# Four PSUM banks for scores and two for turned weights, the latent mask inside the rotary product, and GpSimd's splits in the softmax half

## The reference, cut to what matters

```python
# stick-breaking, strictly causal
z = q @ k.T * 64 ** -0.5
log_rem = where(causal, log_sigmoid(z) - z, 0)
w = where(causal, exp(log_sigmoid(z) + reverse_exclusive_cumsum(log_rem)), 0);  out = w @ v
# latent head: visible is by chunks of 64 tokens
s = (q_nope @ k_nope.T + q_rope @ k_rope.T) * 96 ** -0.5
s = where(k_pos // 64 <= q_pos // 64, s, lowest)
out = softmax(s) @ v
```

## Time and profile before

| | before |
|---|---|
| median of 3 runs | 2409.52 us |
| the profiled execution's own time | 2408.51 us |
| its span | 2406.7 us |
| granted TensorE clock, mean | 0.963 |
| TensorE products busy | 2178.7 us (91%) |
| TensorE weight loads busy | 1817.9 us (76%) |
| VectorE busy | 1348.9 us (56%) |
| ScalarE busy | 1277.0 us (53%) |
| GpSimd busy | 893.4 us (37%) |

### The profile page before, as it was taken

The page is one execution under the profiler, slowest core; times in us unless marked ns, Lnnn a source line. Parts: engine busy times, 40 slices in busy tenths (PEclk is TensorE's granted clock), DMA queues, the critical chain, the costliest instruction groups (busy, mean ns, idle before and its releaser), DMA issues. The chain is left out here.

```text
span 2406.7 us, 39504 instructions
## 1 busy us (share of the span) xinstructions
PE 2178.7 (91%) x12100; PEld 1817.9 (76%) x12100; DVE 1348.9 (56%) x2780; ACT 1277.0 (53%) x2616; POOL 893.4 (37%) x922
## 2 busy tenths in 40 slices
PE   6999998999989799789999999999999993999998
PEld 1888886999988477558686878787877771778886
DVE  3232332300128333278888888888888863667783
ACT  2222232311113333268888888888888873567553
POOL 0000000000000000164858585858585744656673
PEclk9999998999999999879999999999999995999999
DMA  7433332322347799934343434333333215676772
GB/s 277 138 100 100 96 119 79 127 73 73 120 156 203 232 313 309 280 83 99 72 99 68 100 69 96 75 90 78 85 79 83 62 32 143 191 224 179 218 214 88
DMA packets 296938, 320.10 MB, mean 133 GB/s; under 512 B 88642, under 2 KB 221789, under 8 KB 291827
## 3 DMA queue, kind: packets, MB, share of 16 engines
q1 hardware_dynamic: 292002, 302.00, 44.5%
q10 hardware_dynamic: 2880, 9.05, 1.0%
q0 software_dynamic: 1904, 7.41, 0.8%
HBM read 199.09 MB, written 110.90 MB: 129 GB/s over the span
## 5 line engine op out<-in xcount | busy, mean ns | idle before, releaser
L1437 ACT ACTIVATE pa_whi<-banks 128x512 fp32r<-128x512 f32 (+3 forms) x640 | 341.0, 536 | 119.1 <-PE banks L1675 104.8
L1675 PE MATMUL banks<-ident,pa_p 128*128 128x128 f32 x2176 | 350.0, 276 | 0.0
L1600 POOL TENSOR_TENSOR pa_wlo<-pa_whole,pa_whi 128x512 fp32r<-128x512 f32 (+2 forms) x240 | 276.6, 1171 | 135.2 <-ACT pa_whole L1442 135.0
L1658 PE MATMUL banks<-pa_khi,pa_qst 128*128 128x512 f32 (+3 forms) x640 | 257.8, 403 | 59.7 <-DVE pa_p L1503 51.3
L1675 PEld LDWEIGHTS banks<-ident,pa_p 128*128 128x128 f32 x2176 | 264.3, 141 | 54.3 <-issue 1.5
L1632 PE MATMUL banks<-pa_whi,pa_vst 128*128 128x512 f32 (+3 forms) x640 | 282.1, 441 | 17.4 <-POOL pa_wlo L1600 17.4
L1503 DVE TENSOR_TENSOR_SCAN pa_p<-banks,pa_p,pa_zero 128x512 f32<-128x512 f32 x192 | 246.3, 1283 | 64.4 <-ACT banks L1397 57.1
L1480 DVE TENSOR_TENSOR pa_wlo<-banks,pa_whi 128x512 fp32r<-128x512 f32 (+3 forms) x400 | 234.6, 586 | 28.3 <-ACT pa_whi L1437 27.3
L699 POOL DMA_DIRECT2D gate_ada<-in_ada_w_dram x2 | 1.8, 886 | 641.0 <-DVE qu_wlo L755 641.0
L1659 PE MATMUL banks<-pa_klo,pa_qst 128*128 128x512 f32 (+3 forms) x640 | 238.7, 373 | 0.0
L1632 PE MATMUL banks<-pa_wlo,pa_vst 128*128 128x512 f32 (+3 forms) x640 | 234.0, 366 | 0.0
(11 more groups left out here) (260 smaller groups left out, 5198.4 us busy)
## 6 DMA issues: line engine op xcount, KB each, us to landing
scratch_sb_kT<-ke_kT SPq DMA_DIRECT2D x12, 1024.0 KB, 9.1
scratch_mla_kT<-ke_nT SPq DMA_DIRECT2D x12, 1024.0 KB, 5.1
scratch_mla_v<-ke_v SPq DMA_DIRECT2D x12, 1024.0 KB, 5.4
scratch_gatesT<-co_gates SPq DMA_DIRECT2D x12, 704.0 KB, 11.3
ada<-in_ada_w_dram SPq DMA_DIRECT2D x4, 2048.0 KB, 12.3
pr_x<-in_x_prompt_dram SPq DMA_DIRECT2D x16, 512.0 KB, 18.8
scratch_hT<-pr_hT SPq DMA_DIRECT2D x16, 512.0 KB, 5.1
ke_k<-in_cache_sb_k_dram SPq DMA_DIRECT2D x8, 1024.0 KB, 7.6
```

The source lines that it names most:

```text
L1437: act.activation(whi[:, t % NW, q0:], bank, ACT.Copy).then_inc(hi_done, 1)
L1600: pool.tensor_tensor(wlo[:, t % NW, q0:], whole[:, t % 4, q0:], raw(whi[:, t % NW, q0:]), ALU.subtract).then_inc(pool_lo, 1)
L1658: pe.matmul(bank, qst[job][:, q], khi[job][:, keys], start=True, stop=False)
L1675: y = pe.transpose(ps[:, NS + t % NTB, x * P:(x + 1) * P], probs[g][x][:, i * P:(i + 1) * P], s["ident"][:])
```

## The change

It does four things. `NS` becomes 4 and `NTB` 2. The mask of the latent head gets 16 rows of its own in the rotary operands, one for each tile of 128 tokens (`krst` and `qrst` have 112 rows): key rows hold a very low number for the second 64 tokens of the tile, query rows a one for the first 64, so the rotary product adds the mask and the product with `hide` goes. GpSimd's splits lie in steps 22 to 61, in an order of parts by when the old ones are no longer read, with a semaphore for each of the four pieces; SP's loads move with them. At the start SP loads the mask's rows, and GpSimd copies them (and `own_tile`) where ScalarE and VectorE did before.

```diff
-    NS, NTB, NW = 2, 4, 5
+    NS, NTB, NW = 4, 2, 5
...
-        krst = sb("pa_krst", [3 * ROPE, T], F32R)
-        qrst = sb("pa_qrst", [3 * ROPE, T], F32R)
+        ROWS = 3 * ROPE + TILES
+        krst = sb("pa_krst", [ROWS, T], F32R)
+        qrst = sb("pa_qrst", [ROWS, T], F32R)
...
+        mask_rows = slice(3 * ROPE, ROWS)
+        half_rows = [x[mask_rows, 0:T // 2] for x in (probs[1][3][:], probs[2][2][:], probs[2][3][:], whole[:, 0:2].rearrange("p b n -> p (b n)"))]
+        hidden_keys, blind_queries = half_rows[0:2], half_rows[2:4]
+        own_raw = probs[1][0][:, 0:CH]
...
-        SPLITS = (((0, "v", 1), (6, 10, 14, 18)), ((1, "k", 0), (22, 26, 30, 34)), ((1, "v", 0), (46, 50, 54, 58)),
-                  ((1, "k", 1), (62, 66, 70, 74)))
+        SPLITS = (((1, "k", 0), ((0, 22), (1, 24), (2, 26), (3, 28))), ((0, "v", 1), ((0, 30), (1, 32), (2, 34), (3, 36))),
+                  ((1, "k", 1), ((3, 40), (2, 55), (1, 58), (0, 61))), ((1, "v", 0), ((3, 43), (2, 46), (1, 49), (0, 52))))
+
+        def part_order(name, job):
+
+            return [part for (_, *piece), parts in SPLITS if piece == [name, job] for part, _ in parts]
+
+        def left_by(name, job, part):
+
+            if job:
+                users = [G + k for k in range(G) if size_of(G + k) >= part]
+            else:
+                users = [k for k in range(G) if size_of(k) >= part]
+            return upto(max(users))
...
-                sp.dma_start(raw(krst[:]), d["mla_krT"][:, 0:T]).then_inc(kr_loaded, 16)
-                sp.dma_start(probs[2][3][:, 0:CH], d["const_own_tile"]).then_inc(own_loaded, 16)
+                sp.dma_start(raw(krst[0:3 * ROPE, :]), d["mla_krT"][:, 0:T]).then_inc(kr_loaded, 16)
+                sp.dma_start(own_raw, d["const_own_tile"]).then_inc(own_loaded, 16)
+                for i in range(2):
+                    at = slice(i * T // 2, (i + 1) * T // 2)
+                    sp.dma_start(hidden_keys[i], d["const_hidden_keys"][:, at]).then_inc(own_loaded, 16)
+                    sp.dma_start(blind_queries[i], d["const_blind_queries"][:, at]).then_inc(own_loaded, 16)
...
-                LOADS = {0: (load_k, 0), 18: (load_v, 0), 20: (load_q, 0), 34: (load_k, 1), 58: (load_v, 1), 60: (load_q, 1)}
+                LOADS = {0: (load_k, 0), 20: (load_q, 0), 30: (load_k, 1), 38: (load_v, 0), 54: (load_v, 1), 60: (load_q, 1)}
...
-                act.wait_ge(own_loaded, 16)
-                act.wait_ge(hide_made, 2)
-                act.activation(own_tile[:], probs[2][3][:, 0:CH], ACT.Copy)
-                act.activation(hide[:], probs[2][3][:, CH:CH + P + CHUNK], ACT.Copy).then_inc(const_done, 1)
+                act.wait_ge(const_done, 1)
...
-                hidden = probs[2][3][:, CH:CH + P + CHUNK]
-                dve.memset(hidden, 0.0).then_inc(hide_made, 1)
-                dve.wait_ge(hide_made, 1)
-                dve.memset(hidden[0:1, 0:CHUNK], 1.0)
-                dve.memset(hidden[0:1, P:], -BIG).then_inc(hide_made, 1)
...
-                    if part == 0:
+                    first = part == part_order(name, job)[0]
+                    if not (isinstance(h, int) and h == 0):
+
+                        if name == "v":
+                            wait_apart(pool, mixed, NW + HEAD * h + left_by(name, job, part), passed)
+                        else:
+                            wait_apart(pool, scores, HEAD * (h - 1) + left_by(name, job, part), passed)
+                    if first:
                         loaded, count = ((k_loaded, 32 * (2 * h + job + 1)) if name == "k" else
                                          (v_loaded, 80 * h + (80 if job else 64)))
                         wait_apart(pool, loaded, count, passed)
...
+                wait_apart(pool, own_loaded, 5 * 16, passed)
+                pool.tensor_copy(own_tile[:], own_raw).then_inc(row_made, 1)
+                for i in range(2):
+                    at = slice(i * T // 2, (i + 1) * T // 2)
+                    pool.wait_ge(row_made, 2 * i + 1)
+                    pool.tensor_copy(krst[mask_rows, at], hidden_keys[i]).then_inc(row_made, 1)
+                    pool.wait_ge(row_made, 2 * i + 2)
+                    pool.tensor_copy(qrst[mask_rows, at], blind_queries[i]).then_inc(row_made, 1)
+                wait_apart(pool, row_made, 5, const_done)
...
-                        if t in when and not (on and last):
-                            split(h + on, name, job, when.index(t))
+                        for part, at in when:
+                            if t == at and not (on and last):
+                                split(h + on, name, job, part)
...
-                        mm = pe.matmul(bank, qrst[:, q], krst[:, keys], start=False, stop=(c != g))
-                        if c == g:
-
-                            mm = pe.matmul(ps[:, m % NS, width - CHUNK:width], hide[:, 0:P], hide[:, P:],
-                                           start=False, stop=True)
+                        mm = pe.matmul(bank, qrst[:, q], krst[:, keys], start=False, stop=True)
...
+        "const_hidden_keys": np.where((tile == token // P) & (token % P >= CHUNK), f(-BIG), f(0.0)),
+        "const_blind_queries": ((tile == token // P) & (token % P < CHUNK)).astype(f),
```

More of the change, by code:

```diff
@@ L1175, in prompt_attention_phase @@
         const_loaded, const_done = sm.one("const_loaded"), sm.one("const")
-        kr_loaded, own_loaded, hide_made = sm.one("kr_loaded"), sm.one("own_loaded"), sm.one("hide_made")
+        kr_loaded, own_loaded, row_made = sm.one("kr_loaded"), sm.one("own_loaded"), sm.one("row_made")
         k_loaded, v_loaded, q_loaded = sm.one("k_loaded"), sm.one("v_loaded"), sm.pair("q_loaded")
-        kv_hi, kv_split = sm.one("kv_hi"), sm.one("kv_split")
+        PIECES = (("k", 0), ("v", 0), ("k", 1), ("v", 1))
+        kv_hi, kv_split = ({piece: sm.one(f"{what}_{piece[0]}{piece[1]}") for piece in PIECES} for what in ("kv_hi", "kv_split"))
         scores, sig_done, scan_done, cut_done = (sm.one(n) for n in ("scores", "sig", "scan", "cut"))
@@ L1281, in _ @@
                 sp.dma_start(causal[:], d["const_causal"]).then_inc(const_loaded, 16)
[L1282 to L1283 removed]
+                sp.dma_start(raw(krst[0:3 * ROPE, :]), d["mla_krT"][:, 0:T]).then_inc(kr_loaded, 16)
[4 more added lines that the diff above has]
+                    sp.dma_start(blind_queries[i], d["const_blind_queries"][:, at]).then_inc(own_loaded, 16)
                 def load_k(h, job):
                     if job:
[L1287 to L1289 removed]
+                        wait_apart(sp, kv_split["k", 0], PARTS * (h + 1), passed)
+                    else:
+                        wait_apart(sp, kv_split["k", 1], PARTS * h, passed)
                     k = (d["mla_kT"] if job else d["sb_kT"])[bass.ds(h * HD, HD), 0:T]
@@ L1313, in load_v @@
                     if job:
-                        wait_apart(sp, kv_split, kv_upto(h, "v", 0), passed)
-                    elif not (isinstance(h, int) and h == 0):
-                        wait_apart(sp, kv_split, kv_upto(h - 1, "v", 1), passed)
+                        wait_apart(sp, kv_split["v", 0], PARTS * (h + 1), passed)
+                    else:
+                        wait_apart(sp, kv_split["v", 1], PARTS * h, passed)
                     v = (d["mla_v"] if job else d["new_sb_v_prompt"])[0:T, bass.ds(h * HD, HD)]
@@ L1374, in _ @@
                     step(HEADS - 1, t, True)
-                    if t == 24:
-                        sp.wait_ge(kv_split, kv_upto(HEADS - 1, "v", 1))
+                    if t == 40:
+                        sp.wait_ge(kv_split["k", 1], PARTS * HEADS)
+                        sp.wait_ge(kv_split["v", 1], PARTS * HEADS)
                         for c in range(4):
@@ L1541, in _ @@
                     chunk(0, m)
+                dve.wait_ge(const_done, 1)
                 steps_in_turn(dve, step)
@@ L1571, in split @@
                         pool.tensor_tensor(step_v[:, blk], step_v[:, blk], vraw[:, blk], ALU.subtract).then_inc(v_stepped, 1)
-                        wait_apart(pool, v_stepped, PARTS * h + part + 1, passed)
+                        wait_apart(pool, v_stepped, PARTS * h + part_order(name, job).index(part) + 1, passed)
                     high, low, of = {
@@ L1575, in split @@
                         "v": (vst[job][:, blk, 0:HD], vst[job][:, blk, HD:], (vraw if job else step_v)[:, blk])}[name]
-                    pool.tensor_copy(high, of).then_inc(kv_hi, 1)
-                    pool.wait_ge(kv_hi, kv_upto(h, name, job) - PARTS + part + 1)
-                    pool.tensor_tensor(low, of, raw(high), ALU.subtract).then_inc(kv_split, 1)
-                pool.wait_ge(vlast_lo, 1)
-                pool.sem_inc(kv_hi, PARTS)
-                pool.sem_inc(kv_split, PARTS)
+                    pool.tensor_copy(high, of).then_inc(kv_hi[name, job], 1)
+                    pool.wait_ge(kv_hi[name, job], PARTS * h + part_order(name, job).index(part) + 1)
```

(13 more changed lines are left out.)

14 lines of the change are left out of this document (4 added, 10 removed).

## The result

The changed kernel took 2517.95 us (median of 4 runs, 2513.78 to 2536.57), the kernel before 2409.75 beside it (4 runs): ratio 1.0462 [1.0437, 1.0487], slower, as forecast, and inside the range. The size was +108, not +88. The profiled execution took 2513.78, span 2512.0, mean granted clock 0.963, the same as before.

A forecast was written before the change was run, and what follows sets the result against it. TensorE was taken to bound the softmax half, a cycle of TensorE, ScalarE and VectorE the stick-breaking half. Softmax +48, stick-breaking +42, first steps +3, start -5 gave +88: 2497.5 us as a median, range 2452 to 2540.

The forecast's parts named there:

- Part 1: Softmax half: transposes wait for VectorE's low part of two steps earlier; 5.5 us a head, plus 1.0 at step 21.
- The chain T(22) to T(24): Softmax half: from step 22's transposes through scores, cut and low part to step 24's transposes; 3.33 us against 2.86.
- T(21): Softmax half: step 21's transposes, 1.0 us late because VectorE arrives behind from the stick-breaking half.
- Part 2: Mask moved into the rotary contraction: 16 small products a head go, saving 0.5 us; the taller contraction costs 0.
- Part 3: Stick-breaking half: with four score and two turned banks, transposes wait for every fourth low part; cost 6 us a head.
- the ring: Stick-breaking half: four-step loop from one VectorE low part to the fourth after, 6.97 us; nine come to 59.7 against 53.3.
- Part 4: GpSimd's splits, some 12 us a head, move to the softmax half and fit there; lateness goes, credited 0.
- Part 5: Start: the 20 chunks ahead of step 0 gain from four score banks, -5 us once; constant copies 0 or +3.
- A: Rival: deep score ring wins, scan waits go and stick-breaking half falls to some 55 us; 2358 us, chance 0.05.
- B: Rival: same waits, but VectorE and ScalarE absorb half, 3 us a head in each half; 2453 us, chance 0.11.
- D: Rival: transposes' wait hidden, only the mask's -4 and the start's -5 count; near 2400 us, chance 0.03.
- C: Rival: granted clock falls to 0.50 as TensorE waits in pieces, some +27 us a stick-breaking half; about 2690, chance 0.04.

The follow-up runs named there:

- Own-step order: Changed kernel with VectorE making each step's low part in that step, ahead of the scan or cut; 2387.82 us, ratio 0.9906.
- banks alone: Kernel before with only the bank counts changed, to four for scores and two for turned weights; 2520.3 us, ratio 1.0453.
- three banks each: Changed kernel with three banks for scores and three for turned weights; 2379.71 us, ratio 0.9866.
- own-step order on top: Changed kernel with three score and three turned banks, and VectorE's low part made in its own step; 2372.07 us, ratio 0.984.
- all but the banks: Changed kernel with the old bank counts, two for scores and four for turned weights; 2408.94 us, ratio 0.9984.

## Why the prediction was right, and where its size was off

**Part 1 (two turned banks, softmax half) was right.** The chain T(22) to T(24) was worked out as 3.33 and is 3.33; T(21) waits 1.10 where 1.0 was forecast. With the mask's 0.2 put back the half costs 6.7 against 6.5. Own-step order takes 6.2 of the changed half's 63.95 away, which shows that the chain ran through VectorE's order. The part net of the mask was +6.0 a half and came to +6.4.

**Part 2 (mask) was mis-sized.** On its own the mask's removal is worth 1.06 us a head, above the 1 us that I had named as proof against the step. From the start of the rotary product to that of the transposes TensorE takes 267 ns with the mask product between and 234 without for 512 columns (0.033, my 0.032), and about as much more for 256 and 384 (0.031 and 0.036), but 193 against 113 for 128 columns, a quarter of the sixteen; and with the mask product the transposes behind it take 0.63 to 0.66 us and the mix starts 0.39 to 0.41 after them, without it 0.60 to 0.63 and 0.36 to 0.38. By the 1.06 us of the half it is 0.066 each. I had read one wide chunk. In the changed kernel it hardly matters: beside T's wait it brings 0.2.

**Part 3 (stick-breaking half): the ring was right, its clock wasn't.** From the end of low(a) to the end of low(a+4), us:

| ring | before | predicted | banks alone, clock not fallen | after |
|---|---|---|---|---|
| 63 to 67 | 5.09 | 6.51 | 6.42 | 7.57 |
| 67 to 71 | 6.10 | 6.91 | 7.17 | 7.10 |
| 71 to 75 | 5.88 | 6.51 | 6.42 | 6.42 |
| 75 to 79 | 4.69 | 5.9 | 5.55 | 5.51 |
| 79 to 3 | 7.09 | 6.58 | 6.66 | 6.66 |
| 3 to 7 | 6.35 | 6.91 | 7.09 | 7.09 |
| 7 to 11 | 7.33 | 8.0 | 8.5 to 8.8 | 8.5 to 8.8 |
| 11 to 15 | 5.40 | 6.51 | 6.15 | 6.14 |
| 15 to 19 | 5.23 | 5.98 | 6.41 | 6.33 |
| sum | 53.2 | 59.7 | 60.5 | 61.4 |

(Means of the first six halves. The column "predicted" spreads the text's reductions for narrow chunks over the rings; the sum is the text's.) So 6.4 was worked out, 6 was written, and 7.9 came: 1.1 is the fallen clock in the first ring, 0.6 the ring with the loop's jump (the last half has no jump and a ring of 6.65, so the jump costs 1.8 to 2.1 in the ring, not 1.7), 0.4 the rounding; 0.3 of it came back outside the rings. Over seven halves the 1.9 are 13 of the 20 us that were missing; the softmax halves (3), the start (2) and head 0's first steps (2) are the rest. The first ring is also the one that says most about the mechanism: 5.09 before, as VectorE had work ahead, 6.42 even at the full clock now. The ring 11 to 15 came out at 6.14, under the 6.2 that I had named as proof against the four-step ring; it is one with narrow chunks, where I had 6.5, and the nine together bear the ring out.

**Part 4 (GpSimd)** was credited 0. Its lateness went, as said (17.4 to 4.8 us), and with two score banks nothing was gained: moving the splits and loads cost 1.0 us a half there. That freeing TensorE can make one long wait out of two short ones, and that the clock can fall behind it, was in none of my steps. Beside four and two banks it was the other way round: the changed kernel has one fallen stretch a half, the one with banks alone up to two, which is my reading of the 1.1 us between their halves (mask and start differ too). With three banks each three halves still had such a stretch, with the own-step order on top none.

**Part 5 (start).** The 20 chunks gained 7.9, more than 5 (29.9 us before and with all but the banks, 22.0 with the banks alone and in the changed kernel). In this trace the phase began 4.7 us later (first product 1023.4 against 1018.65); in runs with the same start it began between 1018.6 and 1024.8, so I put that to scatter ahead of the phase and not to the change. The clock stood at its lower level for most of it, where before it stood there throughout; how much of the 7.9 this is, no run separates:

```profile
1031.00:1045.40 14.40, 11.31 (x22) 5.41 (x23) 13.46 (x13) 6.03 (x12) 12.89 (x20) 0.57 0.68 146
```

**The rivals.** A (deep score ring wins) fell: its waits did go, but T's wait decides. It came true in part as soon as the low part was no longer behind the scan: 58.1 us in that half and 2387.8 in all, where it had some 55 and 2358. B (half absorbed) fell: both halves cost their full chains. D fell. C (the clock) happened in small: 1.1 us in each of seven halves, 8 us in all, where I had priced it for whole halves. The Trainium skill ("TensorE: Matmul & The Clock Gate", section "A second HAM failure mode: psum-queue depth-cycling") tells of a clock that goes up and down while the engine idles in small pieces between banks. The trace agrees in that it fell and came back, but not in where: the softmax half, where TensorE waits in small pieces at every second step, stands at 1.00, and in the other half it fell at one wait of 2.42 us, yet not at the longer one at step 13. Of the 19.6 us by which the whole was too small, the 8 us of the clock are the largest share, and that no term of the sum had it was the forecast's gap; the median still lay in the range, whose width for other reasons covered it.

**What stays open.** What makes the clock fall. In the kernel with banks alone the same wait of 2.43 us goes with a fallen clock in heads 1, 3, 4 and 6 and not in 0, 2 and 5, and the one of 3.2 to 3.4 us at step 13 in three halves of six. A version in which GpSimd makes every low part, so that no bank waits for VectorE, wasn't tried; it would need a fourth slot for ScalarE's whole copy, and its price isn't known. No run moves the splits without the loads.

## What to carry to other kernels

Banks are to be divided by who empties them: a bank whose reader stands behind another job in its engine's queue needs to cover that job too, so look at what is ahead of the reader before taking its banks. Where banks are short, put the instruction that frees the short kind first in its engine's queue; the same swap gave 5% with four and two and cost 0.5% with two and four. When a wait goes, ask what the engine arrives at next: with the splits moved, two waits became one, the clock fell near it, and the half took 1.0 us longer in the mean instead of shorter.

## What the runs showed of the hardware

- In the stick-breaking halves the granted clock fell to its lower level for some 3 to 7 us near waits of TensorE of 1.2 to 3.4 us, from 0.9 us before the wait's end to 1.9 behind it, and not every time: waits of 2.42 us had it in seven halves of seven in the changed kernel, waits of 2.43 in four of seven with the banks alone, waits of 3.1 to 3.4 in none of six and three of six. It cost 1.05 us of a ring of 6.4. Waits of 0.2 us at every second step of the softmax half left it at 1.00.
- A 64-column product behind one of 256 to 512 columns took 0.03 to 0.04 us, behind one of 128 columns 0.08; with the slower transposes behind it, it cost 0.066 in the mean (1.06 us for sixteen).
- A score product that starts after a wait takes 0.50 us for 512 columns, as before, 0.40 with work ahead of it, and 0.63 at the lower clock.
